# A two-layer decoder trunk on one core: constant products on TensorE at both ends of stages, and the product for the sum of squares behind the first unit

## The reference

```python
def rmsnorm(x, g):
    y = x * rsqrt(mean(x * x, axis=-1) + 1e-6)
    return y * g

def swiglu(x, w_gate, w_up, w_down):
    return (silu(x @ w_gate) * (x @ w_up)) @ w_down

for l in range(2):
    x = x + 0.5 * swiglu(rmsnorm(x, norm_ffn1[l]), ...)     # 1024 -> 2816 -> 1024
    h = rmsnorm(x, norm_mix[l])
    x = x + (rwkv7_time_mix(h, ...) if l == 0 else nsa_attention(h, shared, ...))
    x = x + 0.5 * swiglu(rmsnorm(x, norm_ffn2[l]), ...)
    if l == 0:
        shared = nsa_shared_kv(x, ...)                      # K and V: plain, rotated, compressed
```

## Time and profile before

| | |
|---|---|
| median of 3 runs | 2675.96 us (2670.57 to 2678.03) |
| profiled execution, its own time | 2677.49 us |
| its span, first to last instruction | 2675.4 us |
| TensorE (PE), matmul busy | 2395.1 us, 90% of the span, 17560 instructions |
| VectorE (DVE) busy | 1599.0 us, 60% |
| ScalarE (ACT) busy | 633.4 us, 24% |
| GpSimd (POOL) busy | 583.7 us, 22% |
| mean granted TensorE clock | 0.946 of full speed |

### The profile page before, as it was taken

How to read it: one execution, slowest core, us unless ns; L and a number is a source line. 1 busy time by engine, 2 the same in 40 slices (tenths; PEclk the granted TensorE clock), 3 DMA queues, 4 the chain that set the end, 5 groups by cost and what they waited for, 6 DMA issues and landing times. The chain is left out here.

```text
span 2675.4 us, 44239 instructions
## 1 busy us (share of the span) xinstructions
PE 2395.1 (90%) x17560; PEld 1940.7 (73%) x17560; DVE 1599.0 (60%) x2144; ACT 633.4 (24%) x1227; POOL 583.7 (22%) x390
## 2 busy tenths in 40 slices
PE   7999987986777769999999699999849998999998
PEld 6888864774665647888877588888638887788887
DVE  6656469945666635656555465656536665565654
ACT  3100012214444422100022210101435552210001
POOL 3212135512122122212130031303101201221213
PEclk9999997997999979999999799999969999999999
DMA  4333322441001013333225433332351201333321
GB/s 129 107 90 102 91 75 63 117 120 46 23 25 31 4 32 95 97 91 108 87 75 166 112 94 95 97 100 71 109 137 30 44 2 42 93 102 94 102 83 67
DMA packets 376084, 217.24 MB, mean 81 GB/s; under 512 B 18896, under 2 KB 359824, under 8 KB 375920
## 3 DMA queue, kind: packets, MB, share of 16 engines
q1 hardware_dynamic: 367792, 199.09, 26.3%
q10 hardware_dynamic: 8128, 15.83, 1.7%
HBM read 199.00 MB, written 15.89 MB: 80 GB/s over the span
## 5 line engine op out<-in xcount | busy, mean ns | idle before, releaser
L143 DVE TENSOR_TENSOR w_lo_ffn<-w_raw,w_hi_ffn 128x1024 fp32r<-128x1024 f32 x272 | 508.7, 1870 | 9.4
L387 POOL TENSOR_TENSOR act_ffn<-gated_ffn,usc_ffn 128x512 f32<-128x512 f32 x88 | 128.1, 1456 | 1007.8 <-ACT gated_ffn L367 1007.8
L367 ACT ACTIVATE gated_ffn<-gsc_ffn 128x512 f32<-128x512 f32 x88 | 55.8, 634 | 1010.2 <-DVE gsc_ffn L292 1010.2
L150 PE MATMUL p_gate_ffn<-hhi_ffn,w_hi_ffn 128*128 128x512 f32 x704 | 278.5, 396 | 7.8 <-DVE hlo_ffn L205 7.8
L292 DVE TENSOR_TENSOR gsc_ffn<-p_gate_ffn,rstd_ffn 128x512 f32<-128x512 f32 x88 | 60.9, 692 | 363.1 <-PE p_up_ffn L152 362.1
L150 PE MATMUL p_down_ffn<-ahi_ffn,w_hi_ffn 128*128 128x512 f32 x704 | 274.9, 391 | 2.4 <-DVE x_res L303 2.4
L151 PE MATMUL p_gate_ffn<-hlo_ffn,w_hi_ffn 128*128 128x512 f32 x704 | 276.9, 393 | 0.0
L152 PE MATMUL p_gate_ffn<-hhi_ffn,w_lo_ffn 128*128 128x512 f32 x704 | 276.8, 393 | 0.0
L150 PE MATMUL p_up_ffn<-hhi_ffn,w_hi_ffn 128*128 128x512 f32 x704 | 274.5, 390 | 2.4 <-DVE w_lo_ffn L143 2.4
L152 PE MATMUL p_up_ffn<-hhi_ffn,w_lo_ffn 128*128 128x512 f32 x704 | 274.6, 390 | 0.0
L151 PE MATMUL p_up_ffn<-hlo_ffn,w_hi_ffn 128*128 128x512 f32 x704 | 274.6, 390 | 0.0
(11 more groups left out here) (346 smaller groups left out, 4372.4 us busy)
## 6 DMA issues: line engine op xcount, KB each, us to landing
w_raw<-in_ffn_w_gate_dram SPq DMA_DIRECT2D x88, 512.0 KB, 3.9
w_raw<-in_ffn_w_up_dram SPq DMA_DIRECT2D x88, 512.0 KB, 3.9
w_raw<-in_ffn_w_down_dram SPq DMA_DIRECT2D x64, 512.0 KB, 3.8
w_raw<-in_ffn_w_down_dram SPq DMA_DIRECT2D x32, 384.0 KB, 3.3
w_raw<-in_rw_w_rkv_dram SPq DMA_DIRECT2D x24, 512.0 KB, 4.2
rkv_scratch<-staged_mix ACTq DMA_DIRECT2D x24, 256.0 KB, 2.4
w_raw<-in_kv_w_dram SPq DMA_DIRECT2D x12, 512.0 KB, 4.8
w_raw<-in_rw_w_o_dram SPq DMA_DIRECT2D x8, 512.0 KB, 5.2
```

Source lines behind the costliest of these rows:

```text
L143: nc.vector.tensor_tensor(lo, raw, fp(hi), ALU.subtract).then_inc(s["w_ready"], 1)
L150: nc.tensor.matmul(out, whi, hi, start=first, stop=False)
L367: nc.scalar.activation(gated[:], gsc[:, j], ACT.Silu).then_inc(s["silu"], 1)
L387: nc.gpsimd.tensor_tensor(act32[:], gated[:], usc[:, j], ALU.mult).then_inc(s["act32"], 1)
```

## The change

A new function `keep_busy` issues n products of two constants (`head_ones` and `ident`, fp32, 128 x 128 each); nothing reads what they write. It is called

- at the start of the three later FFNs, of kv and of q, 6 products, where the product for the sum of squares stood;
- at the end of each of the four FFNs, 11 products, and at the end of each `project_add`, 8 (with a PSUM tile `p_busy` of its own);
- at the end of q, 20 products, and in kv 20 products ahead of the last product into `p_swap_kv`.

The product for the sum of squares moves behind unit 1 in the three later FFNs, and behind unit 0 in kv and q. The mix stage's start, the recurrence and the attention are not touched.

```diff
+def keep_busy(core, out, n):
+    for _ in range(n):
+        core.nc.tensor.matmul(out[:, 0:P], core.head_ones[:], core.ident[:], start=True, stop=True)
...
 def ffn(core, tag, x_gain, w_gate, w_up, w_down, ahead):
...
             if not norm.first:
-                norm.tensor(pe)
+                keep_busy(core, norm.p_ms, 6)
...
-                        if first and norm.first and j == 1:
+                        if first and j == 1:
                             norm.tensor(pe)
...
+            pe.wait_ge(s["ms"], 1)
+            keep_busy(core, norm.p_ms, 11)
...
 def project_add(core, tag, yhi, ylo, weights, ahead):
...
+        p_busy = ps("p_busy", [P, P])
...
+            keep_busy(core, p_busy, 8)
...
 class HeadProjection:
...
-        self.norm.tensor(pe)
+        keep_busy(self.core, self.norm.p_ms, 6)
         for u in range(U + 2):
+            if u == 1:
+                self.norm.tensor(pe)
...
+    def tensor_end(self, pe):
+        pe.wait_ge(self.s["ms"], 1)
+        keep_busy(self.core, self.norm.p_ms, 20)
...
 def queries(...):
             heads.tensor(pe)
+            heads.tensor_end(pe)
...
 def shared_kv(...):
             mm.then_inc(s["c2"], 1)
+            heads.tensor_end(pe)
             pe.wait_ge(s["sqc"], 1)
```

More of the change, by code:

```diff
@@ L1533, in tensor @@
         pe.sem_inc(s["w_free"], SLOTS)
-        self.norm.tensor(pe)
+        keep_busy(core, self.norm.p_ms, 6)
         for u in range(U + 2):
+            if u == 1:
+                self.norm.tensor(pe)
             if u < U:
```

## The result

| | before | after |
|---|---|---|
| median of 20 runs each, one chip | 2676.07 us (2670.57 to 2680.97) | 2681.39 us (2675.76 to 2685.32) |
| ratio, 95% interval | | 1.0017 (1.0010 to 1.0024) |
| profiled execution, its own time | 2677.49 us | 2681.85 us |
| span | 2675.4 us | 2679.9 us |
| mean granted clock | 0.946 | 0.954 |

The account below looks back on a forecast made before the run. TensorE, busy 90% of the span, was taken as the bound, idle at stage-edge barriers; +3.4 + 2.5 + 2.6 + 0.9 - 3.9 - 0.5 = +5.0 us on the 2675.96 median gave 2681, range 2671 to 2689.

Parts of the forecast that it names:

- 20 products at kv's end: End of kv: 4.64 us of products ahead of one ScalarE waits for, less 1.23 us free, +3.4 us.
- 20 products at q's end: End of q: products outlast the last transfer, by 0.5 us at full clock or 4.6 at half; taken as +2.5 us.
- moved product, three FFNs: Three later FFNs: the sum-of-squares product now stands in a dense stream after unit 1, 0.86 us each, +2.6 us.
- moved product, kv and q: After unit 0 in kv and q: hidden if the clock holds, else 0.86 us; half the cases, +0.9 us.
- clock, four edges, finish, mix: Stage edges: a kept clock wins up to 7.8 us (edges 5.3, last stage 2.2, mix 0.3); half taken, -3.9.
- edge from kv to the third FFN: Clock is down there; six dense products ahead of unit 0 might restore it sooner, 0 to 1.4 us; taken as -0.5.
- nothing won: First rival, stage edges: idle pieces lower the clock, +10.2, 2686; with share f won, 10.2 - 9.9f; chance 0.20.
- all won: Rival at the stage edges: the whole clock gain of 8.3 us offsets 8.5 of cost, +0.2, 2676; chance 0.12.
- tails free at kv and q: Rival at kv's and q's ends: the tails cost nothing, 5.9 us less, 2675, or 2670.4 with all won; chance 0.05.
- VectorE late: Rival at unit 4 of three FFNs: 2.3 us of slack fails, each losing up to 1 us more, 2684; chance 0.03.
- the floor: Stage starts: unit 1 waits for its w_lo, so cannot start sooner than 6.36 us after unit 0, whatever the clock.
- my half of 7.8: Four edges, last stage and mix: 7.8 us if all the clock is won; half, 3.9, taken because equal waits went both ways.

Follow-up runs that it names:

- experiment 1: Kernel before, with only the product for the sum of squares moved (behind unit 1 in three FFNs, unit 0 in kv and q), no constant products: 2678.64 us, ratio 1.0010.
- experiment 5: Changed kernel with tails twice as long, 22 products at the FFN ends and 16 at the output projections: 2685.30 us, ratio 1.0036.
- experiment 6: Kernel before with only the tails added, 11 products at the FFN ends and 8 at the output projections: 2676.18 us, ratio 1.0001.
- experiment 8: Kernel before plus tails of 12 ahead of kv and finish, 9 after projections, 4 products before the sum-of-squares product in kv and three FFNs: 2669.78 us, ratio 0.9970.
- experiment 9: Kernel before with only the 20 constant products at the end of kv and of q added: 2679.12 us, ratio 1.0010.
- experiment 4: Changed kernel without the 20s, its starts having 2 constant products and then the product for the sum of squares: 2673.98 us, ratio 0.9987.
- experiment 7: Kernel before with 4 constant products ahead of the product for the sum of squares at the starts, no tails, no 20s: 2672.88 us, ratio 0.9988.

## Why the prediction was right, and where it was not

The number was right (2681 against 2681.4), the sign too. The four cost terms came within 0.9 us each; the term for the clock came near in total by luck.

| term | predicted | the traces |
|---|---|---|
| 20 products at kv's end | +3.4 | +3.6 |
| 20 products at q's end | +2.5 | +2.0 |
| moved product, three FFNs | +2.6 | +2.6, 0.86 each from unit 1's start on (experiment 1) |
| moved product, kv and q | +0.9 | 0 in q; 0.5 in kv with the clock down, in the next row |
| clock, four edges, finish, mix | -3.9 | -3.55: kv 1.1, second FFN 0.35, fourth 1.65, finish 0.45, q 0, mix 0 |
| edge from kv to the third FFN | -0.5 | -1.15 |
| sum | +5.0 | +3.5, the touched stages' +3.4 |

An FFN's gain is its stage's difference less the 0.86 us of the product (+0.51, -0.29 and -0.79, less 0.86 each).

**What held.** The price of a constant product (0.232, measured 0.234 at the full clock; at the half clock 0.39, 21 instructions in 4.1 us, where I had estimated 0.44). The price of the moved product (0.86). That the FFN tails are hidden by POOL's last sum and that nothing more is (experiment 5). That the 20s have no cover but 1.23 us at kv and the last transfer at q. That the reciprocal comes late without harm. The rivals: "nothing won" fell with the clock of 1.00 at three of four edges, "all won" with q's 0 and `finish`'s 0.45, "tails free at kv and q" with ScalarE's 3.35 us, "VectorE late" with unit 4.

**The step that failed: what the clock is worth, edge by edge.** I took half of each edge, because equal waits went both ways, and set unit 1's weights against unit 0's end as the floor. Both halves of that step were off, in opposite directions.

Up to unit 1, everything was won and not half. Unit 1 starts 0.5, 1.4, 2.0 and 1.8 us sooner after its stage's start in after than before (second FFN, kv, q, fourth FFN), where the floor allowed 0.3, 1.4, 1.9 and 1.65; and at the edge from kv to the third FFN 1.3, where I had taken 0.5 even in "all won". The clock was kept at 13 of 16 edges over four kernels, and in after it fell ahead of kv and was back within 1.0 us of unit 0's start, so that unit 1 waited for its weights all the same.

Behind unit 1, part of it was lost again. At q, my largest entry, 2.0 us are won at unit 1 and the stage gains 0: w_lo of unit 1 is not the last floor. Behind it stands ScalarE's square, fed by VectorE, at the same time in both kernels. I had followed the stream to the next wait only, and the one after took everything. In the mix stage (0.3 expected) the clock fell in after and gave 0; where it held, in three other kernels, it gave 0.4. And `finish` gave 0.45 of 2.2, for its clock stayed at 0.51 for 3.5 us. Where the clock held throughout, in experiments 5, 6 and 8, it gave 1.6 from the first transpose to the end, less than the 2.2 of my estimate.

Nearly all won in the second and fourth FFN and in kv, nothing in q and a fifth in `finish` add up to 3.55, near my half of 7.8, and nothing in my reasoning made it so. That is luck.

A slip in the first rival: 1.7 and 8.3 make 10.0 and not 9.9, which leaves its f at 0.22.

**The sum.** In stages the change comes to +3.4, while the medians differ by 5.3. The interval of the ratio, 2.7 to 6.4 us, holds both. What stands between them is not settled: the untouched recurrence and attention together were 1.6 us longer in the profiled run of after, which accounts for the profiled pair and not for twenty runs. Nor do the parts add up cleanly in medians: +2.3 (1), +2.6 (9) and -2.4 (4) make 2.5, each with an interval of 2.5 us to either side. That the sum of my terms came out at the measured value is in part luck.

The Trainium skill ("TensorE: Matmul & The Clock Gate", section "Why this matters for your kernels") says that no PE-idle gap above about 3 us should be left. Where both ends were filled the trace mostly agrees, with 13 of 16 edges held behind pieces of 2.4 to 2.55 and at most 1.8 us. But the same pieces lost the clock at the other three, pieces of 2.4 to 2.6 and 1.7 to 2.2 lost it at all four edges of experiment 6, and a wait of 2.75 lost it inside q. A gap shorter than 3 us is not safe here.

## What to carry to other kernels

Filling idle time with useless work pays only where another engine's finish covers the work and where PE itself is what ends the stretch behind it: follow the stream past the first wait, to the next thing that does not hang on PE. Never put such work ahead of an instruction whose result somebody waits for, and do not move a product that fills an idle stretch for nothing into a dense stream. A fill at the start of a stage, behind a barrier, was worth more here (2.9 us by the medians, interval 0.8 to 5.6) than one at its end alone (0, interval 2.1 us gained to 2.7 lost), though the two intervals overlap. And size such an edit by where the next unit starts, over several edges: when the clock comes back differs between executions of the same code by more than the fill is worth.

## What the runs showed of the hardware that was not expected

- The clock need not be kept to gain: with four more products at the start of a stage it was back 1.1 to 3.0 us after unit 0's start (experiment 7), without any fill 3.0 to 6.1, and the program took 2.9 us less.
- With the same code, the clock came back 5.7 us after unit 0's start of the fourth FFN in the kernel before and 3.0 us after it in experiment 9. That alone is 1.3 us of a stage's length.
- Waits of the same length go both ways. The wait of 2.79 us for the square in q left the clock at 1.00 in after, and one of 2.75 us brought it to 0.50 in experiment 4. Behind the same tail, 2.56 us at the barrier ahead of the mix stage left it up in experiment 6 and 2.55 brought it down in after.
- A faster start can make a stage slower: 93.22 us for q in experiment 4 against 90.73, through a wait that grew from 0.92 to 2.75 us and the clock that was lost in it.
- The transposes of the last stage run at the full clock, 32 in 3.68 us at 1.00 (experiment 8), against 32 in 5.35 us in after at 0.51 for the first 3.5 us. For such transposes through TensorE the Trainium skill ("TensorE: Matmul & The Clock Gate", section "Part 4: PE-mode transpose") says that the full clock doesn't engage. The trace disagrees: in after the granted clock rose from 0.51 to 1.00 while only they ran (window of the changed kernel).

```profile
2670.00:2673.50 3.50, 3.50 (x17) 3.50 (x18) 0.00 (x0) 1.79 (x3) 0.00 (x0) 0.51 0.02 9
2673.50:2675.50 2.00, 1.82 (x17) 1.58 (x15) 0.00 (x0) 1.89 (x4) 0.00 (x0) 1.00 0.81 332
```
